# Every 24th expert weight piece: the last 16 of its 128 partitions go as two transfers of eight partitions each

## The reference

```
def moe_swiglu(h, router_w, w_gate, w_up, w_down):
    logits = (h @ router_w).astype(jnp.float32)
    top_logit, top_idx = lax.top_k(logits, TOP_K)          # TOP_K = 2
    gate = jax.nn.softmax(top_logit, axis=-1)
    ...
    def expert_block(args):
        tok, e = args
        xb = h[tok]
        hid = jax.nn.silu(xb @ w_gate[e]) * (xb @ w_up[e])
        return hid @ w_down[e]
```

## Time and profile before

| | us |
|---|---|
| three runs | 1997.57, 1997.74, 2000.01 |
| their median | 1997.74 |
| the profiled execution, its own time | 1995.88 |
| its span, first to last instruction | 1994.1 |
| mean granted clock of TensorE | 0.991 |
| PE busy | 1911.1 (96%) |
| expert stage on PE, from its first piece to its last | 1140 to 1982 |

### The profile page before, as it was taken

The page is one execution under the profiler, slowest core; times in us unless marked ns, Lnnn a source line. Parts: engine busy times, 40 slices in busy tenths (PEclk is TensorE's granted clock), DMA queues, the critical chain, the costliest instruction groups (busy, mean ns, idle before and its releaser), DMA issues.

```text
span 1994.1 us, 45014 instructions
## 1 busy us (share of the span) xinstructions
PE 1911.1 (96%) x19812; PEld 1235.3 (62%) x19812; DVE 763.8 (38%) x1769; ACT 333.9 (17%) x779; POOL 293.3 (15%) x267
## 2 busy tenths in 40 slices
PE   7999998999999999999998899999999998999997
PEld 5886556578888888886777644435344352444354
DVE  5586647346554455436556621110010111121102
ACT  3005636121000010222455300000000000000001
POOL 0872623000000000067533000000000000000000
PEclk9999999999999999999999999999999999999999
DMA  9224672522212321412202799999999999999997
GB/s 363 86 85 150 231 253 88 179 76 80 90 64 91 100 85 53 160 43 85 85 2 82 302 378 391 408 418 410 417 419 414 419 416 416 394 400 414 418 412 289
DMA packets 134447, 481.83 MB, mean 242 GB/s; under 512 B 11802, under 2 KB 48010, under 8 KB 103402
## 3 DMA queue, kind: packets, MB, share of 16 engines
q1 hardware_dynamic: 130192, 473.99, 60.8%
q0 software_dynamic: 1040, 3.54, 0.6%
q10 hardware_dynamic: 3018, 1.39, 0.2%
HBM read 476.79 MB, written 2.10 MB: 240 GB/s over the span
## 4 chain that ended last, share of the span: by engine, by line
PE 72%; DVE 4%; POOL 3%; DMA 3%; ACT 2%; issue 2%; DVEq 0%; ACTq 0%; POOLq 0%; SPq 0%
PE bank L893 70%; PE bank L896 2%; POOL ring L3823 2%; POOL work L3825 1%; DMA table<-in_moe_w_dram 1%; DMA ring<-in_moe_w_dram 1%; ACT ring L2108 1%; DVE gates L3715 0%; DMA ring<-in_ada_w_dram 0%; POOL work L3821 0%; DVE ring L3102 0%; DVE ring L3121 0%; DVE ring L3089 0%; ACT L2108 0%; DVE hT L3719 0%
## 5 line engine op out<-in xcount | busy, mean ns | idle before, releaser
L893 PE MATMUL bank<-ring,hT 128*32 128x256 f32 (+3 forms) x8544 | 698.8, 469 | 6.5 <-DMA ring<-in_moe_w_dram 3.2
L893 PEld LDWEIGHTS bank<-ring,hT 128*32 128x32 f32 (+1 forms) x8544 | 308.6, 113 | 380.2 <-issue 290.2
L893 PE MATMUL bank<-ring 64*64 64x64 f32 (+5 forms) x4184 | 412.7, 291 | 22.3 <-issue 8.7
L893 PEld LDWEIGHTS bank<-ring 64*64 64x64 f32 (+3 forms) x4184 | 340.1, 156 | 82.5 <-issue 39.2
L893 PE MATMUL bank<-hT,ring 128*128 128x256 f32 (+1 forms) x1448 | 355.9, 402 | 2.7 <-DVE gates L2945 1.2
L893 PEld LDWEIGHTS bank<-hT,ring 128*128 128x128 f32 x1448 | 273.3, 191 | 68.8 <-issue 33.4
L2108 ACT ACTIVATE gates<-bank 128x256 f32<-128x256 f32 (+2 forms) x75 | 36.3, 484 | 732.6 <-PE bank L893 731.1
L3905 POOL DMA_INDIRECT work<-token_rows,moe_index x11 | 10.1, 921 | 735.9 <-PE bank L896 629.5
L3715 DVE TENSOR_TENSOR gates<-gates,bank 128x512 f32<-128x512 f32 (+1 forms) x42 | 25.1, 597 | 227.9 <-PE bank L893 227.9
L3700 DVE SCALAR_TENSOR_TENSOR xT<-bank,mods,xT 128x256 f32<-128x256 f32 x88 | 35.5, 477 | 192.6 <-PE bank L893 192.6
L3754 DVE COPY work<-bank 128x512 f32<-128x512 f32 (+1 forms) x19 | 10.0, 561 | 255.8 <-PE bank L893 255.8
(11 more groups left out here) (284 smaller groups left out, 1590.1 us busy)
## 6 DMA issues: line engine op xcount, KB each, us to landing
ring<-in_moe_w_dram SPq DMA_DIRECT2D x210, 1024.0 KB, 22.0
ring<-in_moe_w_dram SPq DMA_DIRECT2D x116, 768.0 KB, 21.2
ring<-in_ada_w_dram SPq DMA_DIRECT2D x24, 2048.0 KB, 8.5
ring<-in_ffn_w_dram SPq DMA_DIRECT2D x22, 1024.0 KB, 7.7
ring<-in_w_in_dram SPq DMA_DIRECT2D x10, 2048.0 KB, 8.0
work<-in_moe_w_dram SPq DMA_DIRECT2D x15, 1024.0 KB, 23.7
table<-in_moe_w_dram SPq DMA_DIRECT2D x15, 1024.0 KB, 24.6
ring<-in_w_out_dram SPq DMA_DIRECT2D x4, 2048.0 KB, 8.5
```

What stands on the lines that cost most here:

```text
L893: return nc.tensor.matmul(o, w, x, start=start, stop=stop)
```

## The change

Of the 368 pieces the 14 with the numbers 50, 74, 98, 122, 146, 170, 194, 218, 242, 266, 290, 314, 338 and 362 are issued as three transfers in place of one: partitions 0 to 111, then 112 to 119, then 120 to 127. Seven of them have rows of 8192 bytes (74, 122, 170, 194, 242, 338, 362), seven have rows of 6144 bytes (50, 98, 146, 218, 266, 290, 314). The three transfers add 16 each to the piece's semaphore, so `piece_landed` counts two more for each such piece that came before on the same semaphore. The wait for the free place stands ahead of the first of the three. Bytes, places and the order of the pieces stay as they were.

```diff
--- before.py
+++ after.py
@@ -693,16 +693,27 @@
                 return max(fixed_place[at][2], at - PIECE_SEMS + 1, 0)
             return pieces_before(u) + used_up(spill_place, n)
 
+        MORE_LOW = range(50, len(fixed_order), 24)
+        LOW_ROWS = P - 16
+
+        def row_parts(u, n):
+
+            return ((0, LOW_ROWS), (LOW_ROWS, LOW_ROWS + 8), (LOW_ROWS + 8, P)) if is_static(u) and pieces_before(u) + n in MORE_LOW else ((0, P),)
+
+        def more_parts(s, upto):
+            return sum(2 for at in MORE_LOW if at % PIECE_SEMS == s and at <= upto)
+
         def piece_sem(u, n):
             return moe_piece_full[(pieces_before(u) + n if is_static(u) else n) % PIECE_SEMS]
 
         def piece_landed(u, n):
 
             if is_static(u):
-                return 16 * ((pieces_before(u) + n) // PIECE_SEMS + 1)
+                at = pieces_before(u) + n
+                return 16 * (at // PIECE_SEMS + 1 + more_parts(at % PIECE_SEMS, at))
             s = n % PIECE_SEMS
             fixed, each = (len(range(s, count, PIECE_SEMS)) for count in (FIXED, NPIECE))
-            return (u - STATIC) * (16 * each) + 16 * (fixed + n // PIECE_SEMS + 1)
+            return (u - STATIC) * (16 * each) + 16 * (fixed + more_parts(s, FIXED) + n // PIECE_SEMS + 1)
 
         def done_at(u, kind, c):
 
@@ -849,7 +860,8 @@
                     else:
                         we = w1e if kind == "w1" else w3e
                         src = we[:, b, FIRST_COL[c]:FIRST_COL[c] + 4 * STRIP[c]]
-                    sp.dma_start(dst, src).then_inc(piece_sem(u, n), 16)
+                    for lo, hi in row_parts(u, n):
+                        sp.dma_start(dst[lo:hi], src[lo:hi]).then_inc(piece_sem(u, n), 16)
 
             for s in range(2, NSLOT):
                 held.pop(s, None)
```

## The result

| | before | after |
|---|---|---|
| median, us | 1997.65 (4 runs, 1995.03 to 2000.01) | 2087.44 (4 runs, 2085.98 to 2093.7) |
| ratio to before, 95% interval | | 1.0454 [1.0436, 1.0472] |
| profiled execution, us | 1995.88 | 2093.7 |
| its granted clock | 0.991 | 0.973 |
| PE busy, us | 1911.1 | 1947.2 |

The change costs 90 us. The prediction was 1995.5. First the page of the kernel after, to be held against the earlier trace rows: span, DMA busy tenths, GB/s, the queue that carries the weights, and the shares of the chain that ended last.

A forecast was written before the change was run, and what follows sets the result against it. PE was taken as the bound, by 0.4 us at most, its last stretch starting when piece 230 lands. That landing gave -2.2 us, all other terms 0: from the median 1997.74 to 1995.5, range 1993.2 to 2000.0.

The forecast's parts named there:

- What bounds the kernel: PE's work from 1659.49 us on sets the end; the landing of piece 230, first of item 7, sets 1659.49.
- What the split moves: At split pieces, eight engines carry 9 rows and the other eight 7, where each took 8; the late engines are relieved.
- the sum: Over the whole kernel, -2.2 us from piece 230's earlier landing and 0 from the other terms, giving 1995.5 from the median.
- All four rivals: Alternative end times: 1993.9 (chance 0.20), 2001.5 (0.14), 2001.5 (0.04) and 1997.7 us (0.14).
- A row's price: In a saturated stretch a MB costs 38.35 engine-us: 0.314 us for a row of 8192 bytes, 0.236 for 6144.
- Piece 230: At item 7's start, it lands 2.20 us earlier after eight split pieces, and PE follows in full: -2.20.
- The end: At the last piece, PE comes 2.20 us earlier and the landing 3.85; the margin grows by 1.65, PE stays bound: 0.
- rival 2: The engines given more rows hold the last engine, so the final landing bounds the end: +3.8, 2001.5 us; chance 0.14.
- Which engines are late: In the weight stream, half the engines end 2 to 6 us later, and the eight-row transfers go to the other half.
- SP and completion marks: SP's 28 more issues, 9.3 us, hide in its 487.4 us wait: 0; small transfers' marks cost 0, at most 0.1.
- The clock: A half-rate PE stretch at 1661 to 1665 us may be spared or one added: 0, bounds -1.8 and +1.8.
- rival 4: Nothing moves: small rows spread over all 16 engines, or row count doesn't decide the last engine; 1997.7 us, chance 0.14.

The follow-up runs named there:

- shift4: Against the kernel before, 14 pieces load first half rows in all partitions, then second halves by four eight-row transfers to partitions 4+j, 8+j, ... 32+j: 2002.10 us.
- own32: Against the kernel before, 14 pieces load first half rows in all partitions, then second halves by four eight-row transfers to partitions 32+j, 36+j, ... 60+j: 1990.24 us.
- own_from_cross: Against the kernel before, 14 pieces load first half rows, then four eight-row transfers to partitions j, j+4, ... j+28, read from neighbouring HBM rows 8j to 8j+7: 1990.64 us.
- kernel one: Only piece 218 is split, into 112, 8 and 8 partitions, against the kernel before: 2002.62 us, ratio 1.0022.
- block14: The 14 split pieces stand one behind the other, pieces 208 to 221, against the kernel before: 2032.65 us, ratio 1.0163.
- cols3: The 14 pieces go as three transfers cut along the row, each of all 128 partitions, against the kernel before: 1997.44 us, ratio 1.0010.
- up64: Against the kernel before, 14 pieces load first half rows in all partitions, then second halves by four eight-row transfers to partitions 64+j, 68+j, ... 92+j: 2005.93 us.

## Why the prediction was wrong

*What bounds the kernel* was read rightly, and proved a good measure: item 7's start, set by the landing of piece 230, moved in each kernel with what its splits cost.

*What the split moves* is the step that failed. It went: "Of a piece of 128 rows each engine takes 8. Of 112 it takes 7", then priced each row moved at 0.314 or 0.236 us, whichever engine writes it. In that a row was a load on an engine alone. The runs show that it also matters where that engine writes it: shift4 and own32 differ by the partitions of their small transfers alone (and by the rows of HBM that go with them, which own_from_cross shows to be harmless), and by 11.9 us. For the split itself the term that was missing measured 49.3 us up to piece 230, in place of the 2.20 gained, and 90 in all. Neither the sum nor any rival had a term for it. All four rivals counted rows; the dearest stood at 2001.5.

*A row's price* of 38.35 engine-us for a MB is right outside the stretches (418 and 426 GB/s at 1410 and 1430, against 417 in the earlier trace rows) and 77.4 within them. *Piece 230* was to land 2.20 us earlier; item 7, which starts on its landing, started 49.3 later.

*The end*: the margin between the last landing and PE was to grow by 1.65 us. It didn't grow. By the completion marks the last piece is in at 1980.8 before and at 2078.5 after, and its first matmul stands at 1981.11 and 2078.62: 0.3 us, then 0.2. PE still has no idle time in brackets there, so it stayed the bound by as little as before. The stretch at half share or below did get longer. The windows of the kernel after, to be held against the earlier trace rows:

```profile
2062.00:2063.00 1.00, 1.00 (x7) 1.00 (x6) 0.00 (x0) 0.00 (x0) 0.00 (x0) 0.50 0.60 229
...
2074.00:2075.00 1.00, 1.00 (x18) 0.48 (x8) 0.00 (x0) 0.00 (x0) 0.00 (x0) 1.00 0.12 49
```

At 2074 to 2075 the share is 0.12, two engines of 16. The stretch lasts from about 2063 to 2077 here, against 1975 to 1981 before, and I had written that this would speak for rival 2, that the burdened half is late.

*Which engines are late* is a second step that failed, in part. It went from one engine to eight, and the sum then has "the late half is relieved". The completion marks of a split piece settle it, where no split stands before it. Piece 218 of kernel one and piece 208 of block14 both have 20 of their 32 marks in the early group and 12 in the late one. An eight-row transfer leaves eight marks, one for each engine that has a part in it: the queue carries 130416 - 130192 = 224 packets more than before, 16 for each of the 14 pieces. An engine with a row of each eight-row transfer leaves three marks at a piece, any other leaves one. With eight engines in each group (in cols3 the 48 marks of piece 218 divide into 24 and 24) that makes six burdened engines among the early, 6 x 3 + 2 = 20, and two among the late, 2 x 3 + 6 = 12. So six of the eight late engines were relieved, and two were burdened. Rival 2 needed that "one engine of the eight is as late as the latest of the others"; two were at least in their group. The end of the kernel after agrees: the last six marks of piece 362 come in two groups of three (2063.5, 2063.9, 2064.1 and 2065.6, 2066.1, 2066.3), one for each of its transfers, so the two last engines both carry rows of the eight-row transfers. What this costs by itself no run shows; rival 2 put it at 3.8 us, and the larger effect covers it.

*SP and completion marks* at 0: cols3 bears both out, with 28 more transfers and +1.6 us, [-0.06%, +0.26%]. SP's cover shrank from 487.4 us to 238.9.

*The clock* at 0 within 1.8 us: PE was busy for 36.1 us more, and waited for weights in the ring 63.7 us in place of 6.2, that is 57.5 more. The two make 93.6 of the 97.8 us between the profiled executions. Beside waits PE had stretches at the lower clock (granted 0.50 at 2062 to 2063, and from 1660 to 1665 in block14, both above), which make its matmuls longer. I take the 36.1 for a consequence and not for a second cause, since q1's time alone grew by 95 us, and a matmul that takes twice its time while the next piece is still on its way adds nothing to the end. This is argued; no run holds the clock fixed. One slip of no weight: rival 4 with its clock stretch is 1997.7 + 1.8 = 1999.5, not the 2000.0 of the range.

No kernel of these points to one that beats the kernel before. If the shares above hold, a relief of the late half needs rows of its shares written by other engines, and up64 shows what that costs: 448 half rows displaced, 15.7 us against own32, for a relief that the prediction put at 3.85 at most.

## What to carry to other kernels

In a stage like this, where the DMA engines are saturated by transfers of 128 partitions, leave them at all 128; if one must be cut, cut along the row (no cost here, against 90 us for 14 cuts through the partitions). Judge a stretch by GB/s at a full share, or by share times span of a queue with unchanged bytes, never by the share: a busy engine can be one that waits for another. Before pricing a moved row by the engine that is relieved, ask which other resource the row touches, and put that into a rival, even if no row of the profile shows it yet. And one engine says little about the seven beside it: completion marks can be counted.

## What the runs showed of the hardware

- While engines are at a piece cut through its partitions, all 16 are at about half rate, those at work on whole pieces too: 208 GB/s against 418 at 112+8+8, 216 at 64+64. Cuts at 112+16 and 96+32 end at the same time (2085 to 2089 us for all four). When no engine is at the cut piece, the rate is back: 417 GB/s between the two groups in kernel one.
- Eight-row transfers showed no cost of themselves: 56 of them at every fourth partition from 0 to 31, 18 slow half rows of 2240; the same 56 shifted by four partitions, 341.
- Moved by 32 within the lower 64 partitions the small transfers stay fast (own32: 26 slow half rows), moved by 4 or by 64 they don't (341 and 417): as if partitions 32 apart had the same engine.
- Eight engines ran about 5 us ahead of the other eight in the queue at piece 218 of the kernel before; of the late eight, two take rows of the eight-row transfers.
- Which rows of HBM an engine reads makes no difference here: 1990.04 and 1990.64 us with the same partitions and other rows.
- Not settled: why 112+16 costs as much as 64+64, how the price of one split divides into its own rows and the rest, and whether a transfer of 64 whole rows to partitions that suit its engines would be free. No kernel here had one.
